# Strassen's scheme in the up projections of a gated FFN, with the hidden tiles and the residual spilled to DRAM

## The reference

```python
def conv_ffn(h, w_up, conv_w, conv_b, w_down):
    u = dwconv3(h @ w_up, conv_w) + conv_b          # w_up: 1024 x 5632
    gate, val = jnp.split(u, 2, axis=-1)
    return (jax.nn.silu(gate) * val) @ w_down       # w_down: 2816 x 1024

for i in range(2):                                  # x: 1 x 1024 x 1024, float32
    h = rms_norm(x, mixer_norm_g)
    x = x + (diff_attention(h, ...) if i == 0 else short_conv_mixer(h, ...))
    h = rms_norm(x, ffn_norm_g[i])
    x = x + conv_ffn(h, ffn_w_up[i], ffn_conv_w[i], ffn_conv_b[i], ffn_w_down[i])
return rms_norm(x, final_norm_g)
```

## Time and profile before

| | |
|---|---|
| time, median of 3 runs | 2625.18 us (2624.01 to 2626.92) |
| the profiled execution, first to last instruction | 2624.8 us |
| TensorE busy with matmuls | 2517.0 us (96%), 11476 matmuls |
| VectorE, ScalarE, GpSimd busy | 1437.6, 842.2, 750.0 us |
| TensorE's granted clock, mean | 0.987 of 2.4 GHz |
| moved by DMA | 150.5 MB, 57 GB/s |

### The profile page before, as it was taken

One profiled execution on the slowest core, in us unless ns is written; L12 is line 12 of the kernel. 1 busy time (PEld: TensorE's weight loads), 2 busy tenths in 40 slices (PEclk: granted clock), 3 DMA queues, 4 the chain that ended last, 5 costly groups with the idle time before them and its releaser, 6 DMA issues.

```text
span 2624.8 us, 30478 instructions
## 1 busy us (share of the span) xinstructions
PE 2517.0 (96%) x11476; PEld 2059.2 (78%) x11476; DVE 1437.6 (55%) x1148; ACT 842.2 (32%) x1036; POOL 750.0 (29%) x573
## 2 busy tenths in 40 slices
PE   7999789989999999999999899999999999999996
PEld 5788677777778888888888778888888888888884
DVE  7545699999345444444444544444444444444446
ACT  4111388878332222222222321112322222222222
POOL 2122255655342222222222342223322222222220
PEclk9999899999999999999999999999999999999998
DMA  3332321121111111111111111111111111111111
GB/s 119 129 112 96 96 65 51 54 55 57 72 41 49 48 48 48 48 48 48 48 48 48 40 41 50 50 51 42 48 49 48 48 48 48 48 48 48 48 48 64
DMA packets 41933, 150.53 MB, mean 57 GB/s; under 512 B 5024, under 2 KB 5408, under 8 KB 41888
## 3 DMA queue, kind: packets, MB, share of 16 engines
q1 hardware_dynamic: 41888, 149.92, 16.7%
HBM read 133.12 MB, written 16.78 MB: 57 GB/s over the span
## 4 chain that ended last, share of the span: by engine, by line
PE 74%; issue 6%; POOL 5%; DVE 2%; ACT 1%; POOLq 0%; DVEq 0%; ACTq 0%
PE PS L224 72%; POOL Yl L1136 1%; POOL cu L1129 1%; POOL XGh L1094 1%; PE PS L483 1%; POOL Yl L1094 1%; POOL sq L1142 1%; PE PS L506 0%; DVE XGl L274 0%; PE PS L484 0%; PE PS L491 0%; POOL coef L1123 0%; POOL coef L1120 0%; PE PS L245 0%; DVE X L1082 0%
## 5 line engine op out<-in xcount | busy, mean ns | idle before, releaser
L218 POOL TENSOR_TENSOR Wl<-Wraw,Wh 128x1024 fp32r<-128x1024 f32 x196 | 474.6, 2422 | 1618.0 <-ACT Wh L213 1618.0
L224 PE MATMUL PS<-XGh,Wh 128*128 128x512 f32 x2176 | 674.9, 391 | 27.9 <-POOL Wl L218 23.8
L224 PE MATMUL PS<-XGl,Wh 128*128 128x512 f32 x2176 | 672.0, 390 | 0.0
L224 PE MATMUL PS<-XGh,Wl 128*128 128x512 f32 x2176 | 671.8, 390 | 0.0
L213 ACT ACTIVATE Wh<-Wraw 128x1024 fp32r<-128x1024 f32 x196 | 208.0, 1061 | 1174.5 <-PE PS L224 1076.7
L224 PEld LDWEIGHTS PS<-XGh,Wh 128*128 128x128 f32 x2176 | 409.3, 189 | 115.6 <-issue 22.7
L224 PEld LDWEIGHTS PS<-XGl,Wh 128*128 128x128 f32 x2176 | 409.7, 188 | 85.8
L224 PEld LDWEIGHTS PS<-XGh,Wl 128*128 128x128 f32 x2176 | 409.5, 188 | 85.7
L1033 DVE TENSOR_TENSOR X<-PS,X 128x1024 f32<-128x1024 f32 x160 | 193.9, 1222 | 159.0 <-PE PS L224 158.7
L224 PE MATMUL PS<-Hh,Wh 128*128 128x512 f32 x704 | 224.3, 400 | 8.5 <-issue 8.5
L224 PE MATMUL PS<-Hh,Wl 128*128 128x512 f32 x704 | 223.8, 399 | 0.0
(11 more groups left out here) (142 smaller groups left out, 2809.5 us busy)
## 6 DMA issues: line engine op xcount, KB each, us to landing
Wraw<-weights SPq DMA_DIRECT2D x196, 512.0 KB, 3.2
X<-k_scratch SPq DMA_DIRECT2D x28, 256.0 KB, 3.8
X<-q_scratch SPq DMA_DIRECT2D x28, 256.0 KB, 3.8
X<-x_tiles SPq DMA_DIRECT2D x8, 512.0 KB, 9.2
q_scratch<-X SPq DMA_DIRECT2D x8, 512.0 KB, 2.6
v_scratch<-X SPq DMA_DIRECT2D x8, 512.0 KB, 2.6
k_scratch<-X SPq DMA_DIRECT2D x8, 512.0 KB, 3.0
acc<-v_scratch SPq DMA_DIRECT2D x8, 512.0 KB, 3.2
```

The source lines that it names most:

```text
L218: pool.tensor_tensor(Wl[:, s, :], Wraw[:, s, :], Wh[:, s, :].bitcast(F32), ALU.subtract).then_inc(w_lo, 1)
L224: ins = pe.matmul(ps[:, h * HALF:(h + 1) * HALF], w, m[:, h * HALF:(h + 1) * HALF], start=begin, stop=last and w is wl)
```

## The change: what it does

The up projection of a gate tile and a value tile is treated as a 2 x 2 block product: gate and value rows, even and odd k tiles, lower and upper half of the positions. One level of Strassen's scheme in Winograd's form gets it by 7 products of 4 k tiles x 512 positions, where there were 8. The sums of the activations' blocks are made once per layer in the dense stage before (`spread` on ScalarE, `operands` on VectorE; seven operands, `XB`, for each of four k pairs). The sums of the weights' blocks are made per tile pair by GpSimd (`up_sums`), then split (`up_hi` on ScalarE, `up_lo` on GpSimd). The raw weights come in two DMAs, `up_a` and `up_b`, into the low parts. TensorE accumulates in three banks a pair; ScalarE copies three results in between (`copied`: P1, P5, U2), and VectorE adds four (c11, c22, c12, c21). The factor is applied by `normed`, after the blocks are put together.

`XB` takes 112 KB of each partition, so `X` is stored to DRAM in the dense stage and loaded again after the up projections (`x_load`), and each hidden tile is stored (`h_store`) and loaded for the down projection (`h_load`), where it is split (`h_hi`, `h_lo`). The down projection is a stage of its own: 3 chunks of 8, 7 and 7 hidden tiles, each with 8 jobs, 24 additions to `X` a layer in place of 88. The raw and the low part of a weight tile share a buffer now (`Wraw` lies in `Wst`), so a load waits for the job two before it. The squares of this norm are made in place in `X` and added up in `X[:, 0]` (`square_add`). All loops of the FFN and the dense stages are written out, not looped.

```diff
+        Wst = [at(f"Wst{t}", [P, 2, 1024], ER + 8 * K * t, F32R) for t in range(2)]
...
-        def load_tile(eng, n, s):
-            wait(eng, w_lo, n - 1)
-            eng.dma_start(Wraw[:, s, :], weights[bass.ds(n, 1)].rearrange("a p n -> p (a n)")).then_inc(w_in[s], 16)
-        def split_hi(act, n_half, s, done, jobs):
-            wait(act, done, jobs)
+        def load_tile(eng, n, s, cols=1024):
+            wait(eng, tile_done, n - 1)
+            eng.dma_start(Wraw[s][:, 0:cols], weights[bass.ds(n, 1), :, 0:cols].rearrange("a p n -> p (a n)")
+                          ).then_inc(w_in[s], 16)
...
+        def bank(p, role):
+            b = ((0, 1, 4), (2, 3, 5))[p % 2][role]
+            return PS[:, b * HALF:(b + 1) * HALF]
+        def down_slot(j):
+            return slot((0, 3, 2, 1)[j % 4])
...
+            def ffn(l, base, n):
+                f = F
+                for p in range(FT):
+                    if p + 2 < FT:
+                        sp.wait_ge(f["mm"], nth(l, "mm", 7 * p + 4))
+                        up_a(l, p + 2)
+                    if p == FT - 1:
+                        sp.wait_ge(f["mm"], nth(l, "mm", 7 * (FT - 2) + 7))
+                        sp.wait_ge(f["st0"], nth(l, "st", 16))
+                        sp.wait_ge(f["st1"], nth(l, "st", 16))
+                        h_load(l, 0)
+                        h_load(l, 1)
+                        sp.wait_ge(f["st0"], nth(l, "st", 32))
+                        h_load(l, 2)
+                    if p:
+                        h_store(l, p - 1)
+                    sp.wait_ge(f["mm"], nth(l, "mm", 7 * p + 7))
+                    if p + 2 < FT:
+                        up_b(l, p + 2)
+                    if p == 1:
+                        x_load(0)
+                sp.wait_ge(f["st0"], nth(l, "st", 16 * (FT // 2)))
+                for t in range(3, CHUNKS[0][1]):
+                    h_load(l, t)
+                h_store(l, FT - 1)
+                sp.wait_ge(f["st1"], nth(l, "st", 16 * (FT // 2)))
+                for kt in range(1, KT):
+                    x_load(kt)
+                for j in range(len(CHUNKS) * KT):
+                    c, m = divmod(j, KT)
+                    n2 = base + j + 2
+                    if n2 < T_END:
+                        load_tile(sp, n2, n2 % 2, down_cols(n2))
+                    if c + 1 < len(CHUNKS) and m < CHUNKS[c + 1][1] - CHUNKS[c + 1][0]:
+                        h_load(l, CHUNKS[c + 1][0] + m)
+            dense(0, T_WO, 1)
+            ffn(0, T_D0, 1)
+            for n in range(T_CIN, T_COUT):
+                load_tile(sp, n + 2, n % 2)
+            dense(1, T_COUT, 3)
+            ffn(1, T_D1, 3)
             for kt in range(KT):
                 sp.wait_ge(final_out, kt + 1)
                 sp.dma_start(out[kt], X[:, kt, :]).then_inc(stored, 16)
...
+            def up_product(p, o, kps):
+                role = (0, 2, 0, 1, 0, 2, 0)[o]
+                ps = bank(p, role)
+                for kp in kps:
+                    wh, wl = up_weight(p, o, kp)
+                    bh, bl = XB[kp][:, 0, o, :], XB[kp][:, 1, o, :]
+                    begin = kp == 0 and o in (O_A11, O_S1, O_A12)
+                    pe.matmul(ps, wh, bh, start=begin, stop=False, skip_group_check=True)
+                    pe.matmul(ps, wh, bl, start=False, stop=False, skip_group_check=True)
+                    ins = pe.matmul(ps, wl, bh, start=False, stop=kp == KP - 1, skip_group_check=True)
+                return ins
...
+                def first_pair():
+                    early = (0, 1, 2)
+                    pe.wait_ge(f["lo"], nth(l, "lo", 1))
+                    pe.wait_ge(N[n]["x"], KT - 1)
+                    for kp in early:
+                        pe.wait_ge(N[n]["lo"], 2 * kp + 2)
+                        up_product(0, O_A11, (kp,))
+                    up_product(0, O_S1, early)
+                    up_product(0, O_A12, early)
+                    pe.wait_ge(N[n]["lo"], 2 * KP - 1)
+                    up_product(0, O_A11, (3,)).then_inc(f["mm"], 1)
+                    up_product(0, O_S1, (3,)).then_inc(f["mm"], 1)
+                    pe.wait_ge(f["out"], nth(l, "out", 1))
+                    up_product(0, O_S2, early)
+                    pe.wait_ge(N[n]["lo"], 2 * KP)
+                    up_product(0, O_S2, (3,)).then_inc(f["mm"], 1)
+                    up_product(0, O_A12, (3,)).then_inc(f["mm"], 1)
+                def half_pair(p):
+                    pe.wait_ge(f["lo"], nth(l, "lo", 2 * p + 1))
+                    if p == 1:
+                        pe.wait_ge(N[n]["x"], KT)
+                    wait(pe, f["ev"], nth(l, "ev", 4 * p - 4))
+                    up_product(p, O_A11, range(KP)).then_inc(f["mm"], 1)
+                    up_product(p, O_S1, range(KP)).then_inc(f["mm"], 1)
+                    pe.wait_ge(f["out"], nth(l, "out", 3 * p + 1))
+                    up_product(p, O_S2, range(KP)).then_inc(f["mm"], 1)
+                    up_product(p, O_A12, range(KP)).then_inc(f["mm"], 1)
+                for p in range(FT):
+                    if p == 0:
+                        first_pair()
+                    else:
+                        half_pair(p)
+                    pe.wait_ge(f["lo"], nth(l, "lo", 2 * p + 2))
+                    pe.wait_ge(f["out"], nth(l, "out", 3 * p + 3))
+                    up_product(p, O_S3, range(KP)).then_inc(f["mm"], 1)
+                    up_product(p, O_S4, range(KP)).then_inc(f["mm"], 1)
+                    pe.wait_ge(f["ev"], nth(l, "ev", 4 * p + 2))
+                    up_product(p, O_A22, range(KP)).then_inc(f["mm"], 1)
+                    if p == 0:
+                        square_sum(pe, n)
...
+                pe.wait_ge(f["ev"], nth(l, "ev", 4 * (FT - 1)))
+                pe.wait_ge(sum_read, n + 1)
+                down(0, range(0, 3), True, False)
+                pe.wait_ge(w_lo, base + 2)
+                down(1, range(0, 3), True, False)
...
+            def spread(l, n, kt):
+                g, i = G[l], kt // 2
+                act.wait_ge(N[n]["x"], kt + 1)
+                if kt >= 6:
+                    act.wait_ge(tile_done, (T_WO, T_COUT)[l] + KT)
+                dst = XBf[i][:, 1, 0:5:4, :] if kt % 2 == 0 else XBf[i][:, 1, 3:6:2, :]
+                act.activation(dst, X[:, kt, :].rearrange("p (a n) -> p a n", a=2), ACT.Copy, scale=gcol(n, kt)
+                               ).then_inc(g["cp"], 1)
+                if kt % 2 == 0:
+                    act.wait_ge(g["t"], 5 * i + 2)
+                    act.activation(XB[i][:, 0, 0:2, :], XBf[i][:, 1, 0:2, :], ACT.Copy).then_inc(N[n]["hi"], 1)
+                else:
+                    act.wait_ge(g["t"], 5 * i + 5)
+                    act.activation(XB[i][:, 0, 2:7, :], XBf[i][:, 1, 2:7, :], ACT.Copy).then_inc(N[n]["hi"], 1)
...
+                f, s = F, p % 2
+                if part == 0:
+                    act.wait_ge(f["sums"], nth(l, "sums", 4 * p + 2))
...
+            def dense(l, base, n):
                 for kt in range(KT):
-                    w_hi_static(base + kt + 2, dense_done[d], kt + 1)
-                    norm_act(act, norm, kt)
+                    if kt < KT - 2 or kt == KT - 1:
+                        if kt == KT - 1:
+                            spread(l, n, KT - 2)
+                        spread(l, n, kt)
+                        square_in_place(n, kt)
+                    if kt == KT - 1:
+                        square_in_place(n, KT - 2)
+                    w_hi_static(base + kt + 2)
+                    if kt == 4:
+                        up_hi(l, 0, 0)
+                first_hi(l, base)
             dense(0, T_WO, 1)
...
+                    act.activation(Hs[t][:, 0, :], Hf[t][:, :], ACT.Copy).then_inc(f["hh"], 1)
+                act.wait_ge(N[n]["used"], KT - 1)
+                for p in range(FT):
+                    if p:
+                        middle(p - 1, 0)
+                    copied(p, 0, 1, sP1, 1)
+                    if p:
+                        middle(p - 1, 1)
+                    copied(p, 2, 2, sP5, 2)
+                    if p + 1 < FT:
+                        up_hi(l, p + 1, 0)
                     else:
-                        wait(act, f["hl"], 2 * g + ht - 1)
-                        dst = Tv[:, ht, :]
-                    act.activation(dst, raws[kind][:, 1:S + 1], ACT.Identity, bias=ffn_col(l, g, ht, kind, 3),
-                                   scale=ffn_col(l, g, ht, kind, 1)).then_inc(f["mid"], 1)
-                    act.wait_ge(f["conv"], 4 * g + j + 1) if kind == 0 else None
-                    if kind == 0:
-                        act.activation(Tg[:, :], Tg[:, :], ACT.Silu).then_inc(f["silu"], 1)
+                        h_hi(0)
...
+                        gate(p - 1)
+                    copied(p, 0, 3, sU2, 3)
+                    if p == 0:
...
+                def c11(p):
+                    dve.wait_ge(f["mm"], nth(l, "mm", 7 * p + 4))
```

(83 more changed lines are left out.)

589 lines of the change are left out of this document (339 added, 250 removed).

## The result

The changed kernel takes 2702.4 us (median; 2698.1 to 2705.6), the kernel before 2625.4 in the same comparison: a ratio of 1.029, 95% interval 1.0275 to 1.0304. It is slower by 77 us where 158 were forecast; the time lies in the range. TensorE has 528 matmuls less, as counted, and still ends later.

What follows compares the result with a forecast made beforehand. TensorE's matmuls were taken to bound the FFN stages. The terms -119.7 + 118 + 42 + 53 + 5 + 39 + 5 + 26 + 10 - 20 = +158, on 2625.2, gave 2783 us; range 2660 to 2860.

Steps and rivals of the forecast that it cites:

- Work saved, -119.7: TensorE's up projections: 84 matmuls per tile pair in place of 96, 528 fewer at 0.2267 us, -119.7 us.
- The pairs, +118 and +42: Pairs 2 to 20 of each layer: 3.1 us pause before A22, +118 us; slow TensorE clock after it, +42.
- I take the first: Choice for pairs 2 to 20: all 38 last 22.1 us, 3.1 over 19.04, giving +118 us.
- The second end: Alternative for pairs 2 to 20: half last 19.95 us, the others 22.1, giving +76 us in place of +118.
- the turns going VectorE's way every second pair: Rival on the pairs: +76 and the clock stays up, 2679 us; turns or clock milder had chance 0.22.
- The lock: VectorE two-input SBUF instructions and GpSimd SBUF reads exclude each other for whole instructions; `hidden` waits 4.55 us.
- the rival that a long instruction doesn't hold VectorE off: At `hidden` against the 2048-column difference: no blocking, 165 us less than forecast, 2618 us; faster had chance 0.13.
- Start of a stage, +53 and +5: First two pairs of each layer: 16 us TensorE pause and late second pair, +53 us; slow clock after, +5.
- Up to down, +39 and +5: Before the third down job: TensorE idles for weight tile 2 from 22.5 to 42.1, +39 us; clock +5.
- Dense stages, +26 and +10: Dense jobs: weight loads wait for the job two back, pauses on odd tiles, +26 us; clock +10.
- Given back, -20: Last down jobs: earlier waits for VectorE go, -12.5 us and, in layer 1, -7.3; together -20.
- a slower rate as a rival (+27): Up-projection matmuls at 0.234 us in place of 0.2267: 27 us where nothing pauses, some 4 where TensorE does.

Runs made afterwards that it cites:

- experiment 1: Changed kernel with GpSimd's weight differences of 2048 and 1536 columns issued as instructions of 512, nothing else changed: 2649.1 us, ratio 1.009.
- Experiment 5: Changed kernel with GpSimd's two last square additions moved ahead of the last dense tile's split and of first_lo: 2707.7 us, ratio 1.0309.
- Experiment 4: Changed kernel with SP's loads of down tiles 2 and 3 and h tiles 8 and 9 ahead of the x_loads and h_store(21): 2666.2 us, ratio 1.0151.
- Experiment 6: Changed kernel; in dense jobs ScalarE makes the next weights' high part right after spread's first copy, GpSimd splits them before adding the square: 2674.6 us, ratio 1.0191.
- last version: Changed kernel with 512-column GpSimd differences, down and h tiles loaded ahead of the residual, and next dense weights split before the square: 2578.2 us, ratio 0.9817.

## Why the prediction was half right

The sign, the places and the kinds of wait were right; the size, +158 us, was twice the +77 that came. Of the 81 us between, 58 lie in the pairs and 16 in a rate that the sum left out; the rest is small. By its own steps:

- **Work saved, -119.7.** Right: 10948 matmul records against 11476 before, 528 fewer; pair 21, which prepares nothing, took 19.05 us (19.04 predicted).
- **The pairs, +118 and +42: the step that failed.** It reads: "I take the first", that every pair from 2 to 20 is of the long kind. The second end, "half the pairs at 19.95", was the truth: 20 of the 38 are short, 19.8 us and one of 20.55, and 18 are long, 22.5 to 25.0 and 23.8 in the mean. Pairs 2 to 20 took 413.4 us in layer 0 (860.82 to 1274.25) and 412.2 in layer 1, against 361.8 at full rate: +102 in place of +160. That is the prediction's own rival, the turns going VectorE's way every second pair, which with the clock falling lay at 2679 to 2720. The choice hung on 0.1 us between two requests. At an undisturbed boundary VectorE started at 3.14 us (3.5 taken) and GpSimd mostly at 3.6 to 3.8 (3.4 taken), as `up_b` lands after 3.6 us on the page of the changed kernel: 3.2 was read from the weight loads. So VectorE wins the first turn, and the prediction's own remark, that the 1536-column difference then runs into the next pair, is what makes the next one long. Inside a long pair it was close: `hidden` 5.43 us (5.6), pause 3.09 (3.1), its releaser c22. The clock there was under-sized, 1.6 to 1.7 us against 1.1.
- **The lock.** The Trainium skill (SBUF — State Buffer, SBUF: two separate sides) has the two engines exclude each other for a whole instruction. The rows of before showed it for 1024 columns alone; now it holds at 2048 (5.43 and 5.39 us), and experiment 1 shows the converse, 2.13 us with instructions of 512. So the rival that a long instruction doesn't hold VectorE off is refuted.
- **Start of a stage, +53 and +5.** The pause was 16.14 us (16), the first pair's end came 37.97 us after the dense stage's (37.9), the second pair took 28.5 (26.7 plus the 1.7 of the square sum): +53.4 in both layers. No clock comes on top: 37.97 us holds the slow matmuls after the pause, so the extra +5 has no place in the sum. Experiment 5 corrects one thing: the prediction traced the pause to the place of the two `square_add`, but moving them only moves the pause.
- **Up to down, +39 and +5.** Pauses of 17.76 and 18.53 us, 36.3 in sum. From the first x_load to the landed tile it took 13.2 us (1315.94 to 1329.13; 14.5 estimated). The first 21 matmuls after the pause in layer 0 run partly at 1.2 GHz and take 7.44 us for 4.76; twice that loss is the 5.4 of clock. Experiment 4 wins back as much as the two pauses.
- **Dense stages, +26 and +10.** Right within 3 us of 36. From first to last X addition the stage takes 92.8 us in layer 0 and 92.0 in layer 1, against 72.8 and 78.7 before: +20.0 and +13.3, in sum +33.3; a gain of some 5 us by the rate (below) is already in it, so the losses by themselves were some 3 us above the 36. The first pause in layer 0 is 12.18 us (8.1 predicted); after it come 3.12 and 4.17 (3.6 and 4.0 predicted). Experiment 6 gives 28 back.
- **Given back, -20.** Taken as predicted: the waits that it names are gone but for one of 1.3 us, and with it the sum below closes within 1 us.
- **Not in the sum:** the rate of H and Y. The prediction priced a slower rate as a rival (+27); the faster one came: 2112 down matmuls by 7.6 ns make -16 us, and the dense jobs take 10.88 us where they took 11.25.

The sum with these terms: -119.7 + 102.1 + 53.4 + 36.3 + 5.4 + 33.3 + 2.5 - 20 - 16 = +77.3 us, against 77.0 between the medians and 77.1 between the spans. The 2.5 is a later start of the first dense stage (its first addition to `X` at 701.63, before at 699.13); from profile to profile of the changed kernel and its variants that start itself differs by up to 3 us.

Of the 233.0 us on the losing side, runs took back 53 by the length of GpSimd's instructions, 36 by the order of SP's queue and 28 by the order of a dense job on ScalarE and GpSimd. The 53 us at the head of the stages stay; no run here removed them.

## What to carry to other kernels

When arithmetic is moved from TensorE to preparation on VectorE and GpSimd, add up the turns of the two, and look at the longest single instruction of either: it sets what a neighbour waits at the worst moment, and cutting it into pieces of 512 columns bought 53 us net here. When a cost depends on which of two requests comes first by a tenth of a microsecond, look for a feedback from one period to the next before choosing a side, and forecast the mean of an alternation. An honest comparison also evens out the layout: of the last version's 48 us, 22 could be had in the kernel before with a pad of 96 bytes (2604.0 against 2578.2 us), so the scheme, with its three repairs, is worth some 26.

## What the runs showed of the hardware that was not expected

TensorE's rate changes by 3% (0.2267 to 0.2343 us for 512 columns) with a shift of some arrays by 32 to 96 bytes, while a shift of nearly all by 32 leaves it; what about the shift does it stays open. A wait that fixes the order of turns can cost far more than the worst natural order: pairs of 27.5 to 29.0 us against 22.5 to 25.0, since it lets the other engine's long instructions into places where they had not been.
